# First attention of a two-block transformer kernel: eight heads in two groups of four instead of four groups of two

## The reference, cut to what matters

```python
def one_chunk(c):
    qc = lax.dynamic_slice_in_dim(qh, c * CHUNK, CHUNK, axis=1)
    kc = lax.dynamic_slice_in_dim(kp, c * CHUNK, band, axis=1)
    vc = lax.dynamic_slice_in_dim(vp, c * CHUNK, band, axis=1)
    sc = jnp.einsum('blhd,bmhd->bhlm', qc, kc, preferred_element_type=f32) * scale + bias[None]
    sc = jnp.where(key_ok[None, None, None, :], sc, NEG_INF)
    pw = jax.nn.softmax(sc, axis=-1)
    return jnp.einsum('bhlm,bmhd->blhd', pw.astype(vc.dtype), vc)
```

## Time and profile before

| what | value |
|---|---|
| median of three runs | 878.4 us |
| the profiled execution's own time | 878.33 us |
| its span, first to last instruction | 877.0 us |
| busy TensorE | 867.4 us (99%) |
| busy VectorE | 725.4 us (83%) |
| busy ScalarE | 573.4 us (65%) |
| TensorE clock granted, mean of the core | 0.998 of full speed |

### The profile page before, as it was taken

One profiled execution on the slowest core, in us unless ns is written; L12 is line 12 of the kernel. 1 busy time (PEld: TensorE's weight loads), 2 busy tenths in 40 slices (PEclk: granted clock), 3 DMA queues, 4 the chain that ended last, 5 costly groups with the idle time before them and its releaser, 6 DMA issues.

```text
span 877.0 us, 18438 instructions
## 1 busy us (share of the span) xinstructions
PE 867.4 (99%) x7308; PEld 846.6 (97%) x7308; DVE 725.4 (83%) x1168; ACT 573.4 (65%) x851; POOL 2.2 (0%) x10
## 2 busy tenths in 40 slices
PE   9999999999999999999999999999999999999996
PEld 7999989999999999999999999899999999999996
DVE  6788999899988899888887999989788985555554
ACT  7858466675696787664446879677786664444542
POOL 0000000000000000000000000000000000000000
PEclk9999999999999999999999999999999999999999
DMA  8866456566775789989895566754455566666551
GB/s 316 284 197 225 149 164 194 170 191 211 271 243 191 257 290 332 324 299 339 328 336 180 168 220 209 209 166 141 152 166 176 187 201 200 192 194 195 182 161 49
DMA packets 59045, 189.87 MB, mean 216 GB/s; under 512 B 8640, under 2 KB 11088, under 8 KB 58832
## 3 DMA queue, kind: packets, MB, share of 16 engines
q1 hardware_dynamic: 58816, 188.69, 65.0%
q10 hardware_dynamic: 144, 0.00, 0.0%
HBM read 186.57 MB, written 1.05 MB: 214 GB/s over the span
## 4 chain that ended last, share of the span: by engine, by line
PE 91%; ACT 4%; DVE 3%; issue 1%; DMA 1%; SPq 0%; DVEq 0%; ACTq 0%
PE bank L1101 28%; PE bank L1103 27%; PE bank L1104 27%; PE bank L1074 1%; PE bank L1073 1%; PE bank L1072 1%; ACT whi L2048 1%; DMA H<-in_xT 1%; PE bank L1035 0%; DVE wlo L1146 0%; PE bank L1042 0%; PE bank L1038 0%; PE bank L887 0%; PE bank L769 0%; ACT L2252 0%
## 5 line engine op out<-in xcount | busy, mean ns | idle before, releaser
L1146 DVE TENSOR_TENSOR wlo<-raw,whi 128x1024 fp32r<-128x1024 f32 x291 | 353.7, 1221 | 83.2 <-ACT whi L2048 82.6
L2048 ACT ACTIVATE whi<-raw 128x1024 fp32r<-128x1024 f32 x291 | 304.7, 1056 | 169.0 <-PE bank L1104 164.2
L1101 PE MATMUL bank<-Alo,whi 128*128 128x256 f32 x1328 | 371.5, 280 | 0.0
L1103 PE MATMUL bank<-Ahi,wlo 128*128 128x256 f32 x1328 | 367.7, 277 | 0.0
L1104 PE MATMUL bank<-Ahi,whi 128*128 128x256 f32 x1328 | 367.7, 277 | 0.0
L1101 PEld LDWEIGHTS bank<-Alo,whi 128*128 128x128 f32 x1328 | 249.9, 188 | 2.8 <-issue 2.2
L1103 PEld LDWEIGHTS bank<-Ahi,wlo 128*128 128x128 f32 x1328 | 249.5, 188 | 0.4 <-issue 0.2
L1104 PEld LDWEIGHTS bank<-Ahi,whi 128*128 128x128 f32 x1328 | 249.5, 188 | 0.0
L1103 PE MATMUL bank<-Fhi,wlo 128*128 128x256 f32 (+1 forms) x320 | 88.9, 278 | 0.0
L1104 PE MATMUL bank<-Fhi,whi 128*128 128x256 f32 (+1 forms) x320 | 88.9, 278 | 0.0
L1101 PE MATMUL bank<-Flo,whi 128*128 128x256 f32 x256 | 70.8, 277 | 0.0
(11 more groups left out here) (447 smaller groups left out, 1378.3 us busy)
## 6 DMA issues: line engine op xcount, KB each, us to landing
raw<-in_stream SPq DMA_DIRECT2D x298, 512.0 KB, 4.3
arows<-in_ada SPq DMA_DIRECT2D x64, 384.0 KB, 5.2
TB<-in_TB SPq DMA_DIRECT2D x1, 1536.0 KB, 7.2
a8r<-a SPq DMA_DIRECT2D x16, 64.0 KB, 4.2
out<-H SPq DMA_DIRECT2D x4, 256.0 KB, 2.9
bc<-in_bc SPq DMA_DIRECT2D x1, 896.0 KB, 5.7
H<-in_xT SPq DMA_DIRECT2D x1, 512.0 KB, 7.2
mats<-in_mats SPq DMA_DIRECT2D x1, 449.0 KB, 7.2
```

The costliest lines, as they stand in the source:

```text
L1101: pe.matmul(os[j], wh, xl, start=k == 0 and (wide or j == 0), stop=False, skip_group_check=not wide)
L1103: pe.matmul(os[j], wl, xh, start=False, stop=False, skip_group_check=not wide)
L1146: v.tensor_tensor(wlo[:, s % NHL, :], raw[:, s % NRAW, :], whi[:, s % NHL, :].bitcast(F32), ALU.subtract).then_inc(*lo_v.up(s))
L2048: a.activation(whi[:, s % NHL, :], raw[:, s % NRAW, :], ACT.Copy).then_inc(*hi.up(s))
```

## The change

The four head pairs go in two groups (g) of two (q). Their scores go to banks 4 to 7 in one visit. The P of the pair q = 1 lies in `nrm`, where the turned P was; each P is turned within its own tile: transposes write the head's own scores bank, and ACT copies it back over P. The outputs of both pairs share bank 3 in two halves, so that one high part and one low part of 512 columns serve two pairs. The transposes, the copies of the turned P and the product with V take the pair q = 1 first. The taps around it are dealt anew. The number of matmuls stays the same.

```diff
-    "att": ([44, 49, 50.5, 50.5, 55, 56, 56, 61, 62.5, 62.5, 67, 68],
-            [n for h in range(4) for n in (45 + 6 * h, 47 + 6 * h, 51 + 6 * h)],
-            [n for h in range(4) for n in (45 + 6 * h, 49 + 6 * h, 50 + 6 * h)]),
+    "att": ([44, 50, 52.5, 52.5, 58, 60.5],
+            [45, 46, 48, 49, 54, 54, 55, 56, 57, 62],
+            [45, 46, 50, 52, 54, 55, 58, 60]),
...
-TAPS = [3] * 13 + [4] * 2 + [5] * 3 + [3, 2] + [1] * 10 + [2] * 7 + [3] * 11
+TAPS = [3] * 13 + [4] * 2 + [5] * 3 + [3, 2] + [1] * 10 + [3, 4, 3, 3, 1, 1, 1, 1] + [3] * 10
...
-        pbuf = [(P1[:, 0, :], nrm[:, T:T + 384]), (P1[:, 1, :], nrm[:, T + 384:T + 768])]
+        heads = [[P1[:, 0, :], P1[:, 1, :]], [nrm[:, T:T + 384], nrm[:, T + 384:T + 768]]]
...
+                for g in range(2):
+                    w.wait_ge(*drained("aq", g))
+                    w.wait_ge(*drained("ak", g))
+                    for q in range(2):
+                        hp = 2 * g + q
+                        for hf in range(2):
+                            hs = slice(64 * hf, 64 * hf + 64)
+                            b = banks[4 + 2 * q + hf]
+                            if g:
+                                w.wait_ge(*att_s.at("p", hp - 2, hf))
+                            pe.matmul(b[:, 0:128], aq[hs, hp, 0:128], ak[hs, hp, 0:128], start=True, stop=True)
+                            pe.matmul(b[:, 128:384], aq[hs, hp, 128:256], ak[hs, hp, 0:256], start=True, stop=True
+                                      ).then_inc(*att_pe.up("s", hp, hf))
+                    yield
+                    for q in (1, 0):
+                        hp = 2 * g + q
+                        for hf in range(2):
+                            b, p = banks[4 + 2 * q + hf], heads[q][hf]
+                            w.wait_ge(*att_v.at("w", hp, hf))
+                            for j in range(3):
+                                i = pe.transpose(b[:, j * 128:(j + 1) * 128], p[:, j * 128:(j + 1) * 128], ident)
+                            i.then_inc(*att_pe.up("t", hp, hf))
                     yield
...
+                    if g:
+                        w.wait_ge(*att_v.at("lo", 0))
+                    for q in (1, 0):
+                        hp = 2 * g + q
+                        for hf in range(2):
+                            h, pt = 2 * hp + hf, heads[q][hf]
+                            o = banks[3][64 * hf:64 * hf + 64, q * T:(q + 1) * T]
+                            w.wait_ge(*att_s.at("p", hp, hf))
...
+                    w.wait_ge(*att_s.at("hi", g))
+                    v.tensor_tensor(flat(Ylo[1], g), banks[3][:, :], flat(Yhi[1], g).bitcast(F32), ALU.subtract
+                                    ).then_inc(*att_v.up("lo", g))
```

More of the change, by code:

```diff
@@ L369, in build @@
         P1 = s1("P1", [128, 2, 384])
-        stat2 = s1("stat2", [128, 16])
+        stat2 = s1("stat2", [128, 2, 16])
         gat = s1("gat", [128, 2, 16])
@@ L665, in conv @@
             def conv():
-                w.wait_ge(*att_v.at("lo", 3))
+                w.wait_ge(*att_v.at("lo", 1))
                 for n, tag in enumerate(("mean", "var")):
@@ L747, in att @@
             def att():
[L748 to L761, removed]
-                    yield
[L763 to L770, removed]
@@ new lines, in att @@
+                    for q in (1, 0):
[4 more added lines that the diff above has]
+                            w.wait_ge(*att_s.at("p", hp, hf))
+                            pe.matmul(o, av[:, 0, h * 64:(h + 1) * 64], pt[:, 0:256], start=True, stop=False,
+                                      skip_group_check=True)
+                            pe.matmul(o[:, 128:256], av[:, 1, h * 64:(h + 1) * 64], pt[:, 256:384], start=False,
+                                      stop=True, skip_group_check=True).then_inc(*att_pe.up("o", hp, hf))
@@ L934, in ready @@
                 if name == "br2":
-                    w.wait_ge(*att_s.at("hi", k))
-                    w.wait_ge(*att_v.at("lo", k))
+                    w.wait_ge(*att_s.at("hi", k // 2))
+                    w.wait_ge(*att_v.at("lo", k // 2))
                     return Yhi[1][:, k, :], Ylo[1][:, k, :]
@@ L2171, in att @@
             def att():
-                for hp in range(4):
-                    exps(hp, pbuf, stat2, att_v, att_s)
+                for g in range(2):
+                    for q in range(2):
+                        hp, st = 2 * g + q, stat2[:, q, :]
+                        for hf in range(2):
+                            w.wait_ge(*att_v.at("n", hp, hf))
+                            for j, x, y in TT:
+                                i = a.activation(heads[q][hf][:, x:y], heads[q][hf][:, x:y], ACT.Exp,
+                                                 bias=st[:, 8 * hf + 2 + j:8 * hf + 3 + j],
+                                                 accum_out=st[:, 8 * hf + 4 + j:8 * hf + 5 + j])
+                            i.then_inc(*att_s.up("x", hp, hf))
+                        yield
+                    for q in (1, 0):
+                        hp = 2 * g + q
+                        for hf in range(2):
+                            w.wait_ge(*att_pe.at("t", hp, hf))
+                            a.activation(heads[q][hf], banks[4 + 2 * q + hf][:, 0:384], ACT.Copy
+                                         ).then_inc(*att_s.up("p", hp, hf))
                     yield
-                    turned(hp, 6, pbuf, att_s, att_pe)
-                    yield
-                    w.wait_ge(*att_pe.at("o", hp, 1))
-                    a.activation(Yhi[1][:, hp, :], banks[3][:, 0:T], ACT.Copy).then_inc(*att_s.up("hi", hp))
+                    w.wait_ge(*att_pe.at("o", 2 * g, 1))
+                    a.activation(flat(Yhi[1], g), banks[3][:, :], ACT.Copy).then_inc(*att_s.up("hi", g))
                     yield
```

41 lines of the change are left out of this document (33 added, 8 removed).

## The result

| | before | after |
|---|---|---|
| median | 878.41 us (4 runs) | **891.26 us** (4 runs, 890.46 to 891.48) |
| profiled execution, own time | 878.33 us | 891.47 us |
| its span | 877.0 us | 889.9 us |
| granted TensorE clock | 0.998 | 0.998 |

The ratio is 1.0142 with an interval of 1.0125 to 1.016. The forecast was 880.1 with a range of 878.0 to 881.8, so the time lies 9.5 us above the range. The change loses 12.9 us, and the forecast loss was 1.8.

A forecast was written before the change was run, and what follows sets the result against it. TensorE was taken as the bound: its matmuls times their cadence plus the attention's visits. 878.33 - 0.4 (merged visits) + 1.15 + 1.05 (two waits) = 880.1 us, range 878.0 to 881.8.

The forecast's parts named there:

- the single one 0.24: The single matmul of `between` at slab 68 on TensorE, put at 0.24 us both before and after the change.
- Neither wait is won back, since behind it TensorE is the bound: TensorE waits for `weigh` before the transposes at slabs 50 and 58, 1.15 and 1.05 us, both lost for good.
- the first wait: Transposes at slab 50: TensorE, ready at 159.29 us, waits for VectorE's heads of pair 1; 1.15 us lost.
- The second: Transposes at slab 58: TensorE, ready at 187.13 us, waits for VectorE's `weigh`; 1.05 us lost.
- the ledger: Queues of TensorE, ScalarE and VectorE followed by row durations; high part of slab 52 at 156.62 us, for example.
- The visits: Attention's merged TensorE visits: scores 1.93 us, transposes 2 x 1.36, products and scores 3.57, last products 1.85.
- The merging: Fewer, longer attention visits on TensorE: 10.73 us before, 10.31 now, a gain of 0.4 from two returns saved.
- the rival in which each holds ScalarE longer: Table loads between slab 45 and slab 52's high part each hold ScalarE 1.38 us longer: 884.0 us; chance 0.03.
- the taps cost nothing: VectorE's taps, redealt to slabs 50 to 53 and behind 58: no wait for weights, smallest low-part lead 3.5 us.
- the rival in which VectorE falls behind: Bunched scores at 54 and 55 make TensorE wait for weights at slabs 58 to 60: 881 to 883; chance 0.06.
- or a visit that costs other than twice its content plus 0.2: Sign of a wrong prediction, at the merged visits; products and scores were to lie 3.5 to 3.6 us apart.
- if a visit twice as long returns twice as badly: Proviso on the merged visits' return to TensorE's stream: the 0.4 us gain would then be zero.

The follow-up runs named there:

- a_two68: The changed kernel with two of the single `between` matmuls at slab 68 instead of one, nothing else: 881.78 us, ratio 1.0034.
- b_stat: The kernel before with `stat2` declared at twice its size, so that `gat` lies 64 bytes further on: 879.80 us, ratio 1.0016.
- b_no68: The kernel before without the single matmul of `between` at slab 68: 878.66 us, ratio 0.999.
- b_alone69: The kernel before with the single matmul of `between` moved from slab 68 to a visit of its own at slab 69: 887.86 us, ratio 1.0101.

## Why the prediction was wrong, point by point

**The premise failed.** The prediction says that TensorE's time "is the number of its matmuls times their cadence plus what the attention's visits cost it", and takes 0.1133 us from one stretch as that cadence for the whole kernel, before and after. Matmuls were the same in number, so this product was no term in the sum at all. It is the term that moved: about 12 us, by 0.0044 us on some 2680 matmuls more. A visit has two prices: what it takes, which I worked out to hundredths, and the cadence that it leaves behind, which I did not look for. Nor did I compare the cadence in different parts of the trace of before, where 494 slow starts, 58 us of the stream, could have been seen. In the diff the two causes were marginal: the lone matmul at 68 is in the prediction as "the single one 0.24", once in each sum, and the 64 bytes of `stat2` are in none.

**"Neither wait is won back, since behind it TensorE is the bound": both waits came**, and nearly as large as forecast. Timeline of TensorE in the changed kernel around both groups of transposes (the bracket is idle time and whom for):

```profile
161.28 0.28 PE L1107 MATMUL bank<-Yhi,whi 128*128 128x256 f32 x1
...
161.90 1.00 PE L770 MATMUL bank<-mats,nrm 128*128 128x128 f32 x6 [0.34 <-DVE nrm L1443]
162.74 0.82 PE L770 MATMUL bank<-mats,P 128*128 128x128 f32 x6
...
163.75 0.28 PE L1104 MATMUL bank<-Ylo,whi 128*128 128x256 f32 x1
...
188.64 0.28 PE L1107 MATMUL bank<-Ahi,whi 128*128 128x256 f32 x1
...
189.62 1.01 PE L770 MATMUL bank<-mats,nrm 128*128 128x128 f32 x6 [0.70 <-DVE nrm L1443]
...
191.48 0.28 PE L1104 MATMUL bank<-Alo,whi 128*128 128x256 f32 x1
```

From 161.28 to 163.75, less four slow matmuls, is 2.0 us, and twelve transposes unhindered were put at 1.36, so the first wait is about 0.65 against 1.15. The second is 2.84 - 0.47 - 1.36, about 1.0 against 1.05. Part of the wait is not in the bracket, since the visit itself is drawn out while it waits for the second head. The first is smaller because the slow stream behind slab 44 brings TensorE to slab 50 later, with ScalarE and VectorE still on the ledger. By this working (144 matmuls x 4.4 ns = 0.6 us; no run tests it alone) the slow cadence hid about half a microsecond of it. Together 1.65 against 2.2 us forecast, and 1.0 to 1.4 by the times without them.

**The visits.** They cost less than I put down. The scores of two pairs take 144.79 - 142.51 less four slow matmuls of 0.47 together, 1.8 us (forecast 1.93); products and scores 174.13 - 170.34 - 0.47 = 3.3 (3.57); the last products 199.99 - 197.83 - 0.47 = 1.7 (1.85):

```profile
142.51 0.28 PE L1107 MATMUL bank<-Ahi,whi 128*128 128x256 f32 x1
...
144.79 0.28 PE L1104 MATMUL bank<-Alo,whi 128*128 128x256 f32 x1
...
170.34 0.28 PE L1107 MATMUL bank<-Ahi,whi 128*128 128x256 f32 x1
...
174.13 0.28 PE L1104 MATMUL bank<-Alo,whi 128*128 128x256 f32 x1
...
197.83 0.28 PE L1107 MATMUL bank<-Yhi,whi 128*128 128x256 f32 x1
...
199.99 0.28 PE L1104 MATMUL bank<-Ylo,whi 128*128 128x256 f32 x1
```

The lone matmul takes 0.23 (0.24). The merging therefore gained some 1.0 us instead of 0.4 (10.73 less 1.8 + 2.7 + 3.3 + 1.7 + 0.24). Waits of 1.65 less a gain of 1.0 are 0.65, and the slow cadence behind slab 44 and behind 60.5 adds 1.7 (384 matmuls x 4.4 ns): 2.3 of the 2.5 us that were lost between 108 and 221 us. By these terms alone the time would be 878.33 + 0.65 = 879.0, or 879.5 with the half microsecond of the first wait that the slow stream hid; the forecast had 880.1 for the same terms.

**Table loads.** There are 42, as forecast, and the rival in which each holds ScalarE longer fell. ScalarE in the changed kernel:

```profile
156.15 1.28 ACT L2449 ACT_TABLE_LOAD   x1
157.45 0.20 ACT L2449 ACTIVATE spare<-ones 128x1 f32<-128x1 f32 x1
157.56 0.82 ACT L2407 ACTIVATE gates<-bank,cols 128x256 f32<-128x256 f32 x2
158.27 1.06 ACT L2078 ACTIVATE whi<-raw 128x1024 fp32r<-128x1024 f32 x1
```

The next instruction starts 0.02 us after the load's end. The high part of slab 52 came at 158.27 for a forecast 156.62; with the 1.6 us by which the whole kernel was already late at slab 40, the ledger of ScalarE holds to a tenth. The drain of about 1380 ns that the Trainium skill (page ScalarE: Activation LUTs, section "What ACT_TABLE_LOAD costs") puts beside the load is not in these rows either.

**Taps and low parts.** TensorE waits for no low part between 140 and 260 us, so "the taps cost nothing" held, and the rival in which VectorE falls behind did not come.

**A sign that was named and came.** The list of what would make the prediction wrong ends with "or a visit that costs other than twice its content plus 0.2". That came, on the cheap side: the visit of products and scores took 3.3 us where 3.5 to 3.6 was to show it right. The proviso in the sum, "if a visit twice as long returns twice as badly", did not come. Both are about the return to the stream, and both look at the first matmul after it only, not at the thousands behind.

## What to carry to other kernels

Before a sum is made against a bound engine, read its cadence in several parts of the trace, with the starts of the same instruction: 0.1133 against 0.1178 us from start to start is 4% (and the durations, 276 and 281 ns, show only half of it), and no list of waits shows it. When a result is off, line up the same instructions of the two traces and look at where the difference grows; here it grew where nothing had been changed. Here the stream was cheap to repair: the lone small matmul was put beside other work, or doubled. Measure each place, since no rule found here tells it beforehand.

## What the hardware showed that was not expected

- **Two cadences at one granted clock.** With the granted clock at 1.00, the level of 2.4 GHz, matmuls of 256 columns start every 0.113 or every 0.118 us. For back-to-back matmuls the Trainium skill (page TensorE: Matmul & The Clock Gate, section "Wait — 56ns, not 53.3ns?") has about 2.5 ns beside the columns' own time, which would be 109.2 ns here, an estimate; the trace shows neither of its two values to be that.
- **The cadence is chosen on coming back from a visit** and handed on: behind slab 68 it held for 259 us. From slab 8 on it is the same in all traces of the same program up to the first visit that waited for another engine, and can differ behind such a visit (a_two68 and the changed kernel between 160 and 220 us).
- **What turns it is tiny.** 64 bytes in the place of an operand at slab 8 (b_stat, 1.2 us of the median); at slab 68 one matmul alone or two (887.86 against 878.86 us), but not a shift of its operand by 64 bytes there (888.27).
- **Not settled.** What in the chip holds the two states stays open. No plain rule of count fits: a lone matmul leaves the stream fast at slab 40 and slow at 68 or 69; the last products of two pairs, done alone at 60.5, leave it slow in the changed kernel and fast in the one with `gat` in its place and in the one with two matmuls at 68, though these differ only earlier or later in the program (all three have the waits at slabs 50 and 58 ahead); the convolution's visit at slab 73 turned a slow stream fast without the lone matmul (b_no68) and left it slow with it (b_alone69), so there is more to the state than the cadence itself; one more matmul turned slab 44 and did not turn slab 28. Nor was it tried to hold the timing of a visit while its content changes, which would tell the count from the moment of the return.
